# mLSTM row scaling in a hybrid decoder: four column-operand instructions in place of one broadcast product

## What is computed

```python
hm = mlstm_chunkwise(q, k, v, i_pre, f_pre)          # [B, S, 4, 64]
hm = rms_norm(hm, m_norm_w.reshape(M_HEADS, HEAD_DIM)).reshape(B, S, D_M)
hm = (jax.nn.sigmoid(mo.astype(jnp.float32)) * hm).astype(x.dtype)

def rms_norm(x, w):
    xf = x.astype(jnp.float32)
    y = xf * lax.rsqrt(jnp.mean(xf * xf, axis=-1, keepdims=True) + EPS)
    return (y * w.astype(jnp.float32)).astype(x.dtype)
```

## Time and profile before

| | us |
|---|---|
| median of 3 runs | 2660.82 |
| lowest, highest | 2660.06, 2661.84 |
| the profiled execution, own time | 2663.05 |
| its span, first to last instruction | 2661.2 |

### The profile page before, as it was taken

The page is one execution under the profiler, slowest core; times in us unless marked ns, Lnnn a source line. Parts: engine busy times, 40 slices in busy tenths (PEclk is TensorE's granted clock), DMA queues, the critical chain, the costliest instruction groups (busy, mean ns, idle before and its releaser), DMA issues.

```text
span 2661.2 us, 35751 instructions
## 1 busy us (share of the span) xinstructions
PE 2564.2 (96%) x12676; PEld 2065.7 (78%) x12676; DVE 1831.5 (69%) x3002; ACT 1092.6 (41%) x2082; POOL 1225.6 (46%) x764
## 2 busy tenths in 40 slices
PE   6999999999999999999989999999999999999997
PEld 5678866878788888888766788677877888888886
DVE  5689975774866666666656899758657666666666
ACT  4336345764522232332333463457544232332223
POOL 1348311422644555555433583114236555555545
PEclk9999999899999999999989999999999999999999
DMA  4213311621211111111431133125212111111113
GB/s 137 54 44 95 111 56 45 197 91 73 71 48 48 48 47 63 47 62 54 134 99 38 50 96 113 54 76 164 95 64 64 48 48 64 47 59 53 62 47 134
DMA packets 185249, 199.54 MB, mean 75 GB/s; under 512 B 17648, under 2 KB 160624, under 8 KB 185120
## 3 DMA queue, kind: packets, MB, share of 16 engines
q1 hardware_dynamic: 179360, 176.89, 21.4%
q10 hardware_dynamic: 5760, 20.97, 2.1%
HBM read 156.82 MB, written 38.80 MB: 74 GB/s over the span
## 4 chain that ended last, share of the span: by engine, by line
PE 70%; DVE 20%; ACT 4%; issue 3%; POOL 2%; DMA 1%; SPq 1%; DVEq 0%; POOLq 0%; ACTq 0%
PE ps L2529 30%; PE ps L2556 17%; DVE ties L1359 13%; PE ps L941 9%; PE ps L1895 6%; PE ps L1074 1%; PE ps L1065 1%; PE ps L1084 1%; PE ps L1044 1%; POOL resid L2381 1%; ACT pss L1948 1%; DVE catr L2114 1%; DVE form_lo L1507 1%; ACT pm L1945 1%; DVE score L1276 0%
## 5 line engine op out<-in xcount | busy, mean ns | idle before, releaser
L2313 POOL TENSOR_TENSOR ring_lo<-ring_sum,ring_hi 128x512 fp32r<-128x512 f32 x200 | 307.6, 1554 | 472.3 <-ACT ring_hi L2395 472.3
L2529 PE MATMUL ps<-form_hi,ring_hi 128*128 128x512 f32 x1232 | 482.8, 392 | 11.1 <-DVE form_lo L1507 6.4
L2529 PE MATMUL ps<-form_lo,ring_hi 128*128 128x512 f32 x1232 | 481.6, 391 | 0.0
L2529 PE MATMUL ps<-form_hi,ring_lo 128*128 128x512 f32 x1232 | 481.6, 391 | 0.0
L941 PE MATMUL ps<-act_hi,whi 128*128 128x512 f32 x928 | 377.8, 407 | 8.5 <-ACT smr L431 8.4
L2395 ACT ACTIVATE ring_hi<-ring_sum 128x512 fp32r<-128x512 f32 x200 | 125.3, 633 | 617.4 <-DVE ring_sum L2606 617.1
L941 PE MATMUL ps<-act_hi,wlo 128*128 128x512 f32 x928 | 367.0, 395 | 0.0
L941 PE MATMUL ps<-act_lo,whi 128*128 128x512 f32 x928 | 366.7, 395 | 0.0
L1359 DVE TENSOR_SCALAR_CACHE_REDUCE ties<-score,kth 128x384 uint8<-128x384 f32 (+5 forms) x396 | 348.4, 942 | 5.8 <-issue 1.3
L2621 DVE TENSOR_TENSOR yacc<-yacc,ps 128x1024 f32<-128x1024 f32 x160 | 195.3, 1220 | 220.3 <-PE ps L2556 220.3
L643 POOL TENSOR_TENSOR wlo<-raw,whi 128x1024 fp32r<-128x1024 f32 x54 | 131.7, 2438 | 420.6 <-ACT whi L696 420.6
(11 more groups left out here) (333 smaller groups left out, 4599.5 us busy)
## 6 DMA issues: line engine op xcount, KB each, us to landing
raw<-in_w_in SPq DMA_DIRECT2D x56, 512.0 KB, 3.8
ff_raw<-in_w_gate SPq DMA_DIRECT2D x22, 1024.0 KB, 5.4
ff_raw<-in_w_up SPq DMA_DIRECT2D x22, 1024.0 KB, 5.3
ff_raw<-in_w_down SPq DMA_DIRECT2D x22, 1024.0 KB, 5.0
proj_scratch<-stage ACTq DMA_DIRECT2D x40, 512.0 KB, 2.7
wc<-proj_scratch SPq DMA_DIRECT2D x14, 1280.0 KB, 6.8
xmid_scratch<-xres SPq DMA_DIRECT2D x16, 512.0 KB, 2.6
resid<-xmid_scratch SPq DMA_DIRECT2D x16, 512.0 KB, 6.9
```

The lines of the kernel that those rows point to most:

```text
L2313: pool.tensor_tensor(flat_form(ring_lo[slot]), src, flat_form(ring_hi[slot]).bitcast(F32), ALU.subtract)\
L2529: mm = pe.matmul(ps[:, product_bank(r, i), :], w[:, k], a[:, k], start=(k == 0 and m == 0), stop=(k == 3 and m == 2))
```

## The change

In `scale_out` the one product of 4 x 64 columns, whose second input is the four numbers read again and again over 64 columns each, becomes a loop over the four heads. Each head has a `tensor_scalar`: 64 columns times one number a partition, given as a column operand. The semaphore is raised by the fourth. The two waits ahead, the place in the queue, input and output tiles are the same.

```diff
                     v.wait_ge(*m_stat(L, 2 * c + 2))
                     if c:
                         v.wait_ge(*cat_m(L, c))
-                    v.tensor_tensor(heads(catr[:, 0:256], HD), nd[c % 2][:, :, 0:HD], col(M_RS, MH, HD), ALU.mult).then_inc(m_out.sem, 1)
+                    for h in range(MH):
+                        ins = v.tensor_scalar(catr[:, HD * h:HD * (h + 1)], nd[c % 2][:, h, 0:HD], small[:, M_RS + h:M_RS + h + 1],
+                                              None, ALU.mult)
+                    ins.then_inc(m_out.sem, 1)
```

## The result

The changed kernel takes 2684.55 us (median of three runs, 2682.1 to 2687.57) against 2660.82: +23.7 us. The ratio of the runs is 1.0089, its 95% interval 1.0075 to 1.0102. The direction was as forecast, the size was not: +13.5 was forecast, and the time lies above the upper end of the range, 2682. Some of the places where the time went were not foreseen either.

What follows compares the result with a forecast made beforehand. VectorE's queue through the row scaling in the chunk stage was taken to bound the kernel. Pieces 5.6 us, GpSimd at the seams 6.9 and the clock 1 made +13.5, so 2674.3 us, range 2663 to 2682.

Steps and rivals of the forecast that it cites:

- The bound and the stage: Chunk stage, both layers: the chain of waits runs down VectorE's queue through the row scaling, 11.74 us a chunk.
- The pieces: Row scaling: four small instructions cost 0.71 us on VectorE's queue instead of 0.34, +0.37 in 15 chunks, 5.6 us.
- The new form waits like the old: Where the scaling waits for GpSimd today, the first of the four waits as long; that time stays.
- GpSimd gets in at a seam: Between the four scaling instructions a queued GpSimd instruction is served, +2.3 us each time, 6.9 us in all.
- nobody gets in: Rival: VectorE keeps its turn through all four scaling instructions, only 5.6 us are left, 2666.4 us; chance 0.2.
- three events: Chunk 7 of both layers and chunk 3 of the second: GpSimd's w_out remainder cuts in, 2.3 us each.
- The race: Chunks 4 to 6: the prediction said only that GpSimd has finished, with no time for a later meeting.
- The clock: After the three new TensorE stalls: short falls of the granted clock add 0.3 us each, 1 us.
- The rival of the long falls: Each new stall brings a 5 us fall at half clock, 2.5 us each, up to 2681 us; chance 0.15.

Runs made afterwards that it cites:

- the single piece: Scaling as one tensor_scalar over all 256 columns, with the first head's factor for all heads, against the kernel before: 2660.64 us, ratio 0.9992.
- the small delay: Kernel before with extra VectorE work behind the scaling product in every chunk, two runs: four small memsets, 2661.52 us; one reduction of 224 columns, 2672.26 us.

## Why the prediction was wrong, point by point

*The bound and the stage*: right. The table above holds 24.4 of the 24.6 us, all between VectorE and what follows it.

*The pieces*, +0.37 a scaling forecast: +0.31 measured, 15 x 0.31 = 4.7 in place of 5.6 us. The estimate from the Trainium skill's VectorE: DVE Perf Modes, section on the TRN2 errata, would be 90 cycles or 0.094 us a piece; the trace has 0.16, so the rows were the better guide.

*The new form waits like the old*: right, shown by the single piece.

*GpSimd gets in at a seam*: right, and the largest rival against it, that nobody gets in, is out. The size was off in one place: "the first piece goes, GpSimd's 2.35 us come next, and pieces two to four wait for them" holds for chunk 7 of the first layer (+2.4). In chunk 3 all three seams were used, +3.65, because the delay gives GpSimd's next instructions time to fall due. "In chunk 3 of the first layer VectorE later waits 1.02 us for TensorE" held only for as long as the clock fall that made TensorE late; in the changed kernel's profile that fall was 3.4 us long, and the same 4.7 us were paid there. In chunk 7 of the second layer L1724 was just ahead of the first piece, as in chunk 2. Without the pieces' own 0.31 the scalings grew by 3.34, 2.10 and 1.44 us, 6.9 in all. That this is the forecast's sum is luck: one of its three events used three seams, and another used none. In the second layer's chunk 7 the lost race made the scaling late: with L1738 behind the normaliser the first piece goes there and the second takes 2.38 us, as forecast. Not foreseen were the first layer's chunk 3 and chunk 4 of both layers, where the first piece now meets L1745 (0.81 us instead of 0.25, 1.1 us for two).

*The race*: missing, a term put at nothing without a reason. The prediction said of chunks 4 to 6 only "GpSimd has finished", which is true of L1745, and followed the delay no further. The second place down the queue where VectorE and GpSimd meet stood 5 us later with a margin of 0.12 us, smaller than the 0.37 forecast for the pieces. It costs 0.7 us in five chunks (4 and 5 of the first layer, 4 to 6 of the second), and chunk 3 of the second gets it back once: 4 x 0.7 = 2.8 us.

*The clock*: this term failed most. "I add 0.3 us each, 1 us" stood against 3.7 and 3.9 us a layer at the last turn, of which 0.3 is pieces: 7.0 us. The rival of the long falls, given 0.15, is what happened behind chunk 7 of both layers; behind chunk 3 of the second layer the fall was short, 3.4 us. Its price was short too: it priced 5 us at half rate, where the falls behind chunk 7 lasted 10.2, and the first layer's fall of the earlier trace rows, from which it took the 5, itself lasted 13.7 us. Its argument against itself, that "after chunk 7 TensorE reaches its wait for the last scaling early", held for 0.56 us only. I had taken the second layer's short fall as the usual one, with nothing to choose it by.

Sum by these: 4.7 (pieces) + 6.9 (seams) + 1.1 (L1745 in chunk 4) + 2.8 (race) + 7.0 (clock at the stage's end) = 22.5 of 24.4 us. The other 1.9 are in the main the turn of chunk 1 (a clock fall at 467.1 us, absent before) and the first layer's chunks 3 and 4, where the pieces' 4.7 us and the shorter clock fall nearly cancel. Falls of that kind lie differently from profile to profile: the one at 467 us is absent in the profile of the changed kernel run again, and is there with one piece of the new kind and with the small delay, at 467.0 and 467.4 us. So that one is not the change's doing; for the fall in chunk 3 it stays open.

One slip of the chances: by the prediction's own list those for slower add up to 0.78, not 0.77.

## What to carry over

Where two engines take turns at something, each instruction is one turn: cutting one in four gives the other engine three chances to step in, at its full length each. Before adding even 0.3 us to a queue, look down it for the next meeting with the other engine and read its margin; a delay costs itself within the margin, and beyond it itself plus what is left of the other's instruction (0.7 of 1.04 us here). And a wait that puts the other engine's long, unhurried work behind the short urgent one may be worth more than any form of the instruction: here 10 us for five waits a layer.

## What was new of the hardware

A tensor_scalar of 64 columns with a column operand, float32 in SBUF, starts its follower after 0.16 us (a product of 64 columns after 0.14); one of 256 columns after 0.26, so four small ones cost 0.65 where one large costs 0.26. A waiting instruction of GpSimd was served in between even where the pieces follow 0.16 us apart. The Trainium skill's SBUF — State Buffer, section Who interferes with whom, says that whoever issues first has the shared pair for the whole instruction; the trace agrees, with 2.38 us for a piece beside a GpSimd instruction of 2.34. Memsets of one column on VectorE took 0.013 us each on the queue (0.38 us for 30), so they were no means of delay. And idle times of 2.9 to 3.7 us of TensorE in chunk 7 were followed by a fall of the granted clock to 1.2 GHz in ten of ten cases, which made TensorE 2.2 to 3.4 us late at its next meeting with VectorE; of 18 shorter ones, 0.9 to 2.7 us, three were.
